# A hybrid attention encoder layer: the attention output is kept channel-major from the values product to the output product

## The reference, cut to what matters

```
h = rmsnorm(x, norm_mix_pre); z = h @ w_in
oa = fox_fn(qa, ka, va, logf)           # 8 heads x 64, causal, with a forget bias
ob = band_fn(qb, kb, vb)                # 8 heads x 64, own chunk and 8 chunks before it
oa = rmsnorm(oa.reshape(..., 512), gain_out_a)
ob = rmsnorm(ob.reshape(..., 512), gain_out_b)
mix = concatenate([oa, ob], axis=-1) @ w_out
x = x + rmsnorm(mix, norm_mix_post)
hf = rmsnorm(x, norm_ffn_pre)
x = x + rmsnorm((silu(hf @ w_gate) * (hf @ w_up)) @ w_down, norm_ffn_post)
```

## Time and profile before

| | |
|---|---|
| median of three runs | 3069.04 us |
| the profiled execution, its own time | 3073.0 us |
| its span (first to last instruction) | 3071.3 us |
| PE busy | 2891.6 us (94%) |
| DVE, ACT, POOL busy | 1623.1, 1185.2, 714.4 us |
| mean granted TensorE clock | 0.979 of 2.4 GHz |
| `attend` | about 623 to 1321 us of the span |
| `mix_out` | 1322.5 to 1582.1 us |
| `feed_forward` | 1582.1 us to the end |

### The profile page before, as it was taken

The page is one execution under the profiler, slowest core; times in us unless marked ns, Lnnn a source line. Parts: engine busy times, 40 slices in busy tenths (PEclk is TensorE's granted clock), DMA queues, the critical chain, the costliest instruction groups (busy, mean ns, idle before and its releaser), DMA issues. The chain is left out here.

```text
span 3071.3 us, 56744 instructions
## 1 busy us (share of the span) xinstructions
PE 2891.6 (94%) x22817; PEld 2588.8 (84%) x22817; DVE 1623.1 (53%) x3166; ACT 1185.2 (39%) x2097; POOL 714.4 (23%) x664
## 2 busy tenths in 40 slices
PE   7999999979999889979959999999999999999998
PEld 7999999867777666758749999999999997887887
DVE  6222122167668567744467766776676663224443
ACT  5330000067777556644333334333433342223221
POOL 0000000054344123001134534453443430000000
PEclk9999999979999999989979999999999999999999
DMA  5322212152211886445524232333223335335553
GB/s 165 96 71 77 77 62 75 49 158 75 66 35 56 271 285 221 150 163 161 195 81 146 100 105 93 137 107 111 94 95 110 129 110 167 95 94 167 166 168 120
DMA packets 276460, 376.35 MB, mean 123 GB/s; under 512 B 16536, under 2 KB 203944, under 8 KB 264424
## 3 DMA queue, kind: packets, MB, share of 16 engines
q1 hardware_dynamic: 275912, 371.42, 38.1%
q10 hardware_dynamic: 288, 1.31, 0.1%
HBM read 283.52 MB, written 89.15 MB: 121 GB/s over the span
## 5 line engine op out<-in xcount | busy, mean ns | idle before, releaser
L1218 ACT ACTIVATE att_pts<-att_pt 128x384 f32<-128x384 f32 (+3 forms) x472 | 209.6, 483 | 218.8 <-PE att_pt L1102 204.3
L1207 ACT ACTIVATE att_sx<-att_sx,att_nm 128x640 f32<-128x640 f32 (+17 forms) x272 | 264.9, 980 | 7.3 <-DVE att_nm L1341 7.3
L79 PE MATMUL frt_pz<-frt_xhi,frt_hi 128*128 128x448 f32 (+1 forms) x640 | 230.5, 360 | 0.0
L81 PE MATMUL frt_pz<-frt_xhi,frt_lo 128*128 128x448 f32 (+1 forms) x640 | 230.5, 360 | 0.0
L80 PE MATMUL frt_pz<-frt_xlo,frt_hi 128*128 128x448 f32 (+1 forms) x640 | 230.1, 359 | 0.0
L1102 PEld LDWEIGHTS att_pt<-att_eye,att_sx 64*128 64x128 f32 x3296 | 129.4, 139 | 114.6 <-ACT att_pts L1218 65.2
L1102 PE MATMUL att_pt<-att_eye,att_sx 64*128 64x64 f32 x3296 | 166.9, 232 | 53.3 <-ACT att_pts L1218 22.6
L514 DVE TENSOR_TENSOR frt_shared<-frt_pz,frt_rb 128x448 f32<-128x448 f32 (+1 forms) x80 | 48.9, 611 | 313.5 <-PE frt_pz L81 313.5
L1140 PE MATMUL att_po<-att_pts,att_vv 128*64 128x128 f32 x3296 | 212.9, 277 | 0.0
L1140 PEld LDWEIGHTS att_po<-att_pts,att_vv 128*64 128x64 f32 x3296 | 185.7, 139 | 12.2 <-ACT att_pts L1218 8.9
L79 PE MATMUL frt_pv<-frt_hi,frt_xhi 128*128 128x256 f32 (+1 forms) x544 | 157.8, 290 | 19.6 <-DVE frt_lo L446 15.5
(11 more groups left out here) (297 smaller groups left out, 8267.2 us busy)
## 6 DMA issues: line engine op xcount, KB each, us to landing
ahead_first<-mid_act SPq DMA_DIRECT2D x68, 704.0 KB, 6.7
ahead_second<-in_w_gu SPq DMA_DIRECT2D x33, 1024.0 KB, 5.2
ffn_wr<-in_w_gu SPq DMA_DIRECT2D x33, 1024.0 KB, 5.3
att_raw<-out_zT SPq DMA_DIRECT2D x64, 256.0 KB, 3.5
att_bb<-in_cache_ak SPq DMA_DIRECT2D x16, 1024.0 KB, 9.3
att_bb<-in_cache_av SPq DMA_DIRECT2D x16, 1024.0 KB, 9.5
mid_act<-ffn_ao SPq DMA_DIRECT2D x44, 362.0 KB, 2.5
out_zT<-frt_shared SPq DMA_DIRECT2D x64, 224.0 KB, 1.9
```

The lines of the kernel that those rows point to most:

```text
L79: nc.tensor.matmul(out, a_hi(k), b_hi(k), start=(k == 0), stop=False)
L81: last = nc.tensor.matmul(out, a_lo(k), b_hi(k), start=False, stop=(k == kk - 1))
L1207: nc.scalar.activation(sx[n % NSX][:, e, :w], sx[n % NSX][:, e, :w], ACT.Exp, bias=nm[n % NSX][:, e:e + 1], scale=-1.0, accum_out=sums[n % ...
L1218: nc.scalar.activation(pts[G % NPT][:, :, 0:k, 64 * x:64 * x + 64], pt[x][:].rearrange("p (e j q) -> p e j q", e=2, q=64)[:, :, 0:k, :], A ...
```

## The change

Attention's output stays with channels on partitions all the way to the output product.

- `attend`: `turn_out`, the copy to `att_ot`, the inversion and the multiplication of a prompt job are gone; DVE copies `att_po` straight to `att_os`, right after the values product. ACT writes each job's row sums to a column of one tile (`sums`, 128x256). After the last turning PE turns that tile (two transposes), DVE takes one reciprocal of 128x256 (L1382 of the new file), and SP stores it to a new scratch, `mid_recips`. A stream job keeps its own reciprocal and folds its heads by one product with 64 columns in place of four with 128; one store in place of four, in pieces of 64 bytes.
- `mixT` now holds rows of channels. o(x) is loaded with a channel on each partition (8 pieces of 512 bytes), up to three tiles ahead, and with it the reciprocals, each row spread over 64 partitions by the load (`rs`, another 512 KB per tile). POOL multiplies the one by the other (`scaled`, 128x1024).
- `high` and `low` split that product; `turn_o`, `normed` and the squares' row sums are gone. The group norms' sums over channels now need PE: ACT squares 128x1024, DVE adds twice (128x512 and 128x256), PE multiplies by a column of ones (`group_sums`, two products with 2 columns).
- The output product is made apart for each group, in four PSUM banks (half c, group g). ACT takes out group 0 with its scale (`group_a`), DVE adds group 1 with its own (`group_b`), a pair for each half; `first_sum` then reads the sum from SBUF.
- `feed_forward`: `acts(1)` and `high_a(1)` move from the midst of the down weights to behind the last of them.

```diff
                 def values(n, g):
...
                     if g == 0 and n >= 2:
-                        pe.wait_ge(s_ev, n - 1)
+                        evicted(pe, n - 2)
...
-                def turn_out(n):
-                    pe.wait_ge(s_ot, n + 1)
...
-                    for x in range(2):
-                        r = slice(64 * x, 64 * x + 64)
-                        last = nc.tensor.matmul(po[n % 2][r, P:2 * P], ot[n % 2][:, r], eye[:], start=True, stop=True,
-                                                skip_group_check=True)
-                    last.then_inc(s_to, 1)
+                def fold_out(n):
+                    pe.wait_ge(s_ot, JOBS[n][1] + 1)
+                    nc.tensor.matmul(po[n % 2][:, P:P + CH * NQ], ot[:], fc[:].rearrange("p c t -> p (c t)"), start=True, stop=True,
+                                     skip_group_check=True).then_inc(s_to, 1)
...
+                def evict(n):
+                    after(dve, s_os[n % NOS], stores_ahead(n))
                     if is_stream(n):
...
                     dve.wait_ge(s_pv, T0[n + 1])
-                    nc.vector.tensor_copy(ot[n % 2][:], po[n % 2][:, 0:P]).then_inc(s_ot, 1)
+                    nc.vector.tensor_copy(os_[n % NOS][:], po[n % 2][:, 0:P]).then_inc(s_ev, 1)
+
+                def invert_sums():
+                    dve.wait_ge(s_st, 1)
+                    dve.wait_ge(s_plo, 8 * (NPAIR - 1))
+                    nc.vector.reciprocal(raw[0][:, 0:2 * P], S[0][0][:, 0:2 * P]).then_inc(s_rc, 1)
...
                 for x in range(NT + 3):
-                    if x + 1 < NT:
-                        load(x + 1)
+                    if real(x + 1):
+                        load_x(x + 1)
+                    if real(x + 3):
+                        load_o(x + 3)
+                        load_recips(x + 3)
...
+                def scaled(x):
+                    pool.wait_ge(l_o[x % 3], 16 * (x // 3 + 1))
...
+                    nc.gpsimd.tensor_tensor(o[x % 3][:], o[x % 3][:], rs[x % 2][:], ALU.mult).then_inc(s_on, 1)
...
-                product(x, 0)
-                    if real(x + 1):
-                        turn_o(x + 1)
+                        for g in range(2):
+                            product(x, 0, g)
...
+                    if real(x + 1):
+                        group_sums(x + 1)
...
                 for x in range(NT + 2):
                     if real(x - 1):
-                        resid(x - 1)
-                    if real(x - 1):
-                        resid_add(x - 1)
-                    if real(x + 2):
-                        variance(x + 2)
-                        normed(x + 2)
+                        group_b(x - 1, 1)
+                    if real(x):
+                        variance(x)
                     if real(x + 1):
                         low(x + 1)
+                    if real(x - 1):
+                        resid(x - 1)
+                        resid_add(x - 1)
+                    if real(x):
+                        group_b(x, 0)
+                    if real(x + 1):
+                        group_sum(x + 1)
...
                         for q in range(12, 16):
                             down_weights(q)
-                        acts(1)
...
                 for q in range(18, NJ):
                     down_weights(q)
+                acts(1)
                 up_done(sp)
```

More of the change, by code:

```diff
@@ L772, in slot_count, with evicted @@
             return -(-k // 2) if is_stream(n) else k
+        def evicted(eng, n):
+            streams = sum(is_stream(x) for x in range(n + 1))
+            if is_stream(n):
+                eng.wait_ge(s_es, streams)
+            else:
+                eng.wait_ge(s_ev, n + 1 - streams)
         def masked_bias(n):
@@ L1446, in mix_sems @@
     l_o = [m.sem(f"o{u}") for u in range(3)]
+    l_r = [m.sem(f"recips{u}") for u in range(2)]
     l_x = [m.sem(f"x{u}") for u in range(3)]
     s_ahead = m.sem("ahead")
-    l_o0 = m.sem("first_o")
     s_gains = m.sem("gains_late")
@@ L1586, in hidden @@
                     nc.scalar.activation(h[x % 2][:], x1[x % 3][:], ACT.Copy, scale=r2[x % 2][:, 0:1]).then_inc(s_h, 1)
-                act.dma_start(o[0][:, GW:], mix_rows(t)[0:P, GW:]).then_inc(l_o0, 16)
-                squares(0)
+                for e in range(2):
+                    rows = bass.AP(recips.tensor, recips.offset + e * SEQ, [[0, 64], [2 * SEQ, KD], [1, P]])
+                    act.dma_start(rs[0][64 * e:64 * e + 64], rows).then_inc(l_r[0], 16)
                 act.wait_ge(s_g, 16)
@@ L1643, in _ @@
             def _(pe):
-                def turn_o(x):
-                    pe.wait_ge(s_on, x + 1)
-                    if x >= 1:
-                        pe.wait_ge(s_ol, x)
-                    for k in range(KD):
-                        last = nc.tensor.transpose(po[:, k * P:(k + 1) * P], o[x % 3][:, k * P:(k + 1) * P], eye[:])
-                    last.then_inc(s_to, 1)
                 def turn_h(x):
@@ L1685, in _ @@
                     if real(x):
-                        product(x, 1).then_inc(s_y, 1)
+                        for g in range(2):
+                            product(x, 1, g)
+                    if real(x + 1):
+                        group_sums(x + 1)
             @block.vector
             def _(dve):
-                def variance(x):
-                    dve.wait_ge(s_sq, 2 * x + 2)
-                    nc.vector.tensor_scalar(ss[x % 2][:], ss[x % 2][:], 1.0 / GW, EPS, ALU.mult, ALU.add).then_inc(s_var, 1)
@@ L1705, in hidden, with group_b @@
+                def group_b(x, c):
+                    dve.wait_ge(s_ta, 2 * x + c + 1)
+                    dve.wait_ge(s_y, 4 * x + 2 * c + 2)
+                    if x >= 2:
+                        dve.wait_ge(s_x1, x - 1)
+                    nc.vector.scalar_tensor_tensor(y[x % 2][:, c * HALF:(c + 1) * HALF], py[c][1][:], r[x % 2][:, 1:2], ta[c][:],
+                                                   ALU.mult, ALU.add).then_inc(s_yb, 1)
                 def hidden(x):
@@ L2447, in encoder @@
         ahead = Ahead(nc, late)
-        mix_out(nc, t, mix, ffn.sems, ahead)
+        mix_out(nc, t, mix, ffn.sems, ahead, recips)
         feed_forward(nc, t, up, down, ahead)
```

337 lines of the change are left out of this document (184 added, 153 removed).

## The result

The changed kernel takes 3089.48 us against 3069.04, each the median of five executions: the ratio is 1.0059, with a 95% interval of 1.0047 to 1.0071. It is slower by 0.6%, where 1.6% faster was forecast. (One of its five executions, 3260 us at a lower clock, was disturbed and is left out of the ratio.)

A forecast was written before the change was run, and what follows sets the result against it. PE was taken to set the pace in attend and mix_out's middle, loads at mix_out's start. Terms -33 - 3 + 0 + 3 - 8 - 5.8 + 0.7 - 1.5 = -47.6 us gave 3025.4, median 3021; range 3003 to 3040 us.

The forecast's parts named there:

- The step that failed: mix_out's loads in 512-byte pieces, priced at 262 GB/s at full share: 2.0 us each, 6 us for three at the start.
- fourth rival: mix_out: spread loads taking four times as long set the pace at 15.2 us a tile; 3069 us or more, chance 0.03.
- mix_out, each tile: PE loses turn_o and gains two small products, 12.94 to 12.34 us; 0.5 us per tile taken, 8 us in all.
- up to 2.6: mix_out: extra us per tile if DVE's resid_add passes stand until POOL's scaled is done, making the chain 12.6 us.
- the 5 us that the prediction worked out from the rule alone: mix_out: if each tile's chain pays the whole 2.6 us, the stage gains little more than 16 x 0.3 us.
- Tile 10: mix_out: o(x) asked for up to three tiles ahead, before load_ahead, so the 5.8 us of extra tile distance go.
- The start: mix_out: o(1) and two tiles of reciprocals load ahead of the last weight slab; +3 us, ends 0 and +7.
- attend, prompt jobs: turn_out's 0.27 us of PE goes from 128 jobs, 34.6 us; 33 us taken, bounds 20 and 58.
- -33 and -3: attend: 33 us from prompt jobs, 3 us from streams, where one 64-column product replaces four with 128 (0.2 us x 16).
- attend's end: Two PE transposes and a DVE reciprocal of 1.9 us beside the last values products; 0 us, at most +2.
- feed_forward: Down product: the 5.94 us wait goes, PE then stands 4 to 5 us before tile 1; -1.5 us, bounds -6 and +2.
- The sum: Whole kernel: all terms together -47.6 us against the profiled execution's 3073.0, giving 3025.4; expected median 3021 us.

The follow-up runs named there:

- e3: Changed kernel with row sums laid out so a spread load reads one row of 4096 bytes 64 times, not eight of 512 (long pieces); 3045.48 us, ratio 0.9919.
- e4: Kernel before with only the feed_forward edit, the second tile's activations loaded and rounded behind all weight chunks; 3073.09 us, ratio 1.0008.
- e6: Kernel with long pieces and the old feed_forward, plus DVE copying the second half of every turned group in attend; 3036.3 us, ratio 0.9884.
- e7: Kernel with long pieces and the old feed_forward, each cache-block load but the first two moving half its bytes; 3030.56 us, ratio 0.9865.
- e8: Kernel before the change, each cache-block load but the first two moving half its bytes; 3059.45 us, ratio 0.996.
- e15: Changed kernel with one padding row per head in the reciprocals' tensor, so repeated rows stand 17408 bytes apart, not 16384; 3045.26 us, ratio 0.9909.
- e2: Changed kernel with spread loads of the same form reading rows of mixT, every byte once; 3043.9 us, ratio 0.9916.
- e12: Changed kernel with spread loads reading distinct rows of mixT, each once, all multiples of 16384 bytes apart; 3045.56 us, ratio 0.9915.
- e10: Changed kernel with spread loads reading distinct rows of mixT, a partition's eight pieces 65536 bytes apart; 3048.87 us, ratio 0.9931.
- e9: Changed kernel with spread loads reading eight rows of mixT 64 times each, the rows 8704 bytes apart; 3039.82 us, ratio 0.9902.
- e14: Changed kernel with spread loads reading eight rows of mixT 64 times each, the rows 4096 bytes apart; 3052.06 us, ratio 0.9936.
- e13: Changed kernel with spread loads reading eight rows 64 times each, 16384 bytes apart, from mixT instead of the reciprocals' tensor; 3061.95 us, ratio 0.9974.

## Why the prediction was wrong, by its own steps

**The step that failed** is in the start and the tiles of `mix_out`: "The down product's stretch, whose loads are such pieces, moves 102 GB/s at a share of 0.39, so 262 GB/s at full share: 2.0 us each". A pair of loads of reciprocals took 8.4 us (2 x 4.2), not 2.0. The nearest row had the same piece size but not the same places. With 8.4 us, a tile's DMA work is 8.4 + 1.5 (o) + 3 x 1.3 (x, x1, hT) = 13.8 us, by the distances between landings; the tiles took 14.0 on average. So the DMA engines, put at 9 us and "under 12.3", became what sets the pace. The prediction's fourth rival said just this, with the price (four times as long) and the point from which it decides (5 us a pair); its chance of 0.03 rested on "Nothing in the trace shows such a load", and that absence was read as evidence against. The rival's time, "3069 us or more", held only the tiles; the start cost 20 us as well, for behind these loads the weights waited too.

**mix_out, each tile.** With the loads mended, PE set the pace: 12.28 us in place of 12.94, the end that PE alone would set being 12.34. What rows 10 showed, a DVE pass that stands until POOL's is done, is there too. e3, POOL and DVE side by side:

```profile
1441.54 2.40 POOL L1656 TENSOR_TENSOR mix_o<-mix_o,mix_rs 128x1024 f32<-128x1024 f32 x1
1441.61 3.40 DVE L1779 SCALAR_TENSOR_TENSOR mix_wr<-mix_wr,mix_r,mix_g_post 128x1024 f32<-128x1024 f32 x1 [0.65 <-POOL mix_r L1676]
1445.04 1.23 DVE L1785 TENSOR_TENSOR mix_wr<-mix_wr,mix_xr 128x1024 f32<-128x1024 f32 x1
```

`resid_add` takes 3.40 us where it took 1.28: 2.1 us more, of the "up to 2.6" in the prediction. (In the changed kernel itself all 17 take 1.28: `scaled` waits for its reciprocals and runs at other times.) It cost nothing, since PE, which sets the pace, has no idle time beside it. So the 0.1 us per tile taken off for it (0.5 in place of 0.6) was too careful, and the 5 us that the prediction worked out from the rule alone, with each tile's chain paying in full, missed more; 16 x 0.66 = 10.6 us were gained. By the Trainium skill (SBUF — State Buffer, Who interferes with whom), a DVE instruction with two SBUF inputs contends with a GpSimd instruction that reads SBUF, and the ports they share are an exclusive lock. The rows agree: DVE ends 1.07 us after POOL's 2.40.

**Tile 10.** The 5.8 us go, as said, in every kernel with quick loads. With the loads of the changed kernel the queue was never ahead, and the stall grew to some 10 us (24.37 us less a tile's 14).

**The start.** +3 was taken; with long pieces it is +4.2 (38.7 against 34.5), with slow loads +20.

**attend, prompt jobs.** -33 and -3 were forecast, -20 came (15 to 22 over the eleven kernels that share this stage but for the order of the row sums, 17.8 in the mean; the kernel of e4, whose `attend` is the old one, ends it 2.7 us later than the kernel before, so 2 to 3 us of this are noise). The mechanism was right, and two sizes were off. In a wide pair the term was 16 x 0.27 = 4.3 us; the pairs went from 94.0 to 91.9, 2.05 us less. Counted step by step over two pairs, a product behind scores takes 154 ns for its second step instead of 103, be it of `turn_out` or of the values. `turn_out` had paid these 0.05 us 16 times; now the values products do: 0.8 us. The other 1.5 us are a difference: PE's waits grew by 1.0 us per pair (15.3 us from 730 to 1000 us before, 18.3 after), and 0.5 is not accounted for. e6, which takes copies off ACT, gets more than these back, so ACT is what ended last. And in the first eight streams the DMA engines set the pace, so that next to nothing was gained there (0.7 us, against 6.0 with half the loads, e7 and e8); the prediction read the share of 0.45 over the whole stage, and rows by stretch would have shown 0.92. PE without `turn_out`, scores and then values:

```profile
850.14 0.42 PE L1071 MATMUL att_s<-att_kh,att_ql 64*128 64x512 f32 x2
850.49 1.53 PE L1146 MATMUL att_po<-att_pts,att_vv 128*64 128x128 f32 x24
```

**attend's end.** The reciprocal took 1.76 us (1.9 was estimated). It was nearly hidden: the last values product ends at 1298.28, and its eviction, behind the reciprocal on DVE, starts at 1298.60:

```profile
L1382 DVE RECIPROCAL att_raw<-att_s 128x256 f32<-128x256 f32 x1 | 1.8, 1758 | 0.5 <-PE att_s L1160 0.5
```

**feed_forward.** The stall moved as described; its size was off, 7.0 us in e4, 7.4 in the changed kernel and up to 7.9 in others, in place of the 4 to 5 foreseen. The next wait, for the low part of the activations into `ffn_z`, grew from 1.9 to 3.2 us in the changed kernel (1.8 in e4); the prediction did not have it. So the stage takes +0.8 us (e4), +1.6 (changed kernel) and up to +2.9 (e15) in place of -1.5.

**The sum, mended:** for long pieces -17 (attend, e3) + 4.2 - 10.6 - 5.8 + 0 + 2.4 = -27, which is the difference of the spans, 3071.3 - 3044.3. The failed step cost, against e3, 28.8 us in the tiles (12.1 + 16.7) and 15.8 at the start (54.5 - 38.7): 44.6 us, and this alone turned a gain of 27 into a loss. (`attend` and `feed_forward` are 4 us shorter in the changed kernel than in e3; they differ by as much between executions of kernels that share them.)

**What stays open:** what it is that repeated reads of rows 16384 bytes apart meet in, in the memory or on the way to it; why a load of the same form and distance costs 4.2 us from `recips` and 3.3 from `mixT`; which other distances are slow; and why the DMA engines stand at a share of 0.23 at the start and at 1.02 later with the same 50 GB/s.

## What to carry to other kernels

Price a load by its addresses too, not only by its piece size: here a broadcast that reads eight short rows 4096 or 16384 bytes apart cost two to four times as much as with other distances, and a row of padding or longer pieces avoided it. When no row of a trace is like a new load, keep the bad end of its cost in the range with a real chance, and ask what waits behind it in its queue; here the weights did. And read the share of the DMA engines stretch by stretch before crediting a gain on PE: here, where it was 0.92, a freed PE gained 0.7 us, and 6.0 once the loads were halved.

## What the runs showed of the hardware

- One load of 512 pieces of 512 bytes costs 1.0 to 1.1 us if no row is read twice, 8704, 16384 or 65536 bytes apart alike (e2, e12, e10); with eight rows read 64 times each it costs 1.2 us at 8704 bytes (e9), 1.3 at 17408 (e15), 2.4 at 4096 (e14) and 3.3 to 4.2 at 16384 (e13, changed kernel).
- While it runs slowly, other loads hardly move: from 1306 to 1313 us of the changed kernel ACT's queue, with the first reciprocals, moved 0.38 MB and SP's 0.01 (56 GB/s in all), and slab 0 of the weights, asked for at 1303.57 in SP's queue, landed at 1317.33.
- A DVE pass of 1.28 us with SBUF inputs takes 3.40 when POOL's pass of 2.40 with SBUF inputs starts 0.07 us ahead of it (e3).
- Rows of 4096 bytes read by 64 partitions at once are not slow: 284 GB/s from 1365 to 1370 us of e3, where the changed kernel had 50.
